# Norms of the later layers: squares added in pairs on GpSimd before TensorE sums them

## The reference

```python
def rms_norm(x, g):            # over the 1024 channels of each token
    return x * rsqrt(mean(x * x) + EPS) * g

for l in range(2):
    h = rms_norm(x, mix_pre_g[l])
    ...                        # latent attention, gating unit, differential attention
    x = x + rms_norm(mix, mix_post_g[l])
    h = rms_norm(x, mem_pre_g[l])
    x = x + rms_norm(memory_cross_attention(h, mem_n, ...), mem_post_g[l])
    h = rms_norm(x, ffn_pre_g[l])
    x = x + rms_norm(conv_ffn(h, ...), ffn_post_g[l])
```

## Time and profile before

| | |
|---|---|
| runs | 1940.42, 1940.86, 1935.62 us |
| median | 1940.42 us |
| profiled execution | 1938.43 us |
| its span, first to last instruction | 1936.6 us |
| mean granted TensorE clock | 0.967 of full |
| TensorE matmul busy | 1811.5 us |
| VectorE, ScalarE, GpSimd busy | 508.0, 422.8, 74.8 us |

### The profile page before, as it was taken

One profiled execution on the slowest core, in us unless ns is written; L12 is line 12 of the kernel. 1 busy time (PEld: TensorE's weight loads), 2 busy tenths in 40 slices (PEclk: granted clock), 3 DMA queues, 4 the chain that ended last, 5 costly groups with the idle time before them and its releaser, 6 DMA issues.

```text
span 1936.6 us, 24878 instructions
## 1 busy us (share of the span) xinstructions
PE 1811.5 (94%) x10310; PEld 1409.7 (73%) x10310; DVE 508.0 (26%) x1143; ACT 422.8 (22%) x907; POOL 74.8 (4%) x72
## 2 busy tenths in 40 slices
PE   4987878799999999999999999999999999899997
PEld 2674757566666665678678888888887688788886
DVE  3749432400100100022430312121135312212113
ACT  1532211211110110121442221111224522211112
POOL 0251000100000000010000100000000000000000
PEclk9988889799999999999999999999999999899999
DMA  9111256299999999983322323444433133234420
GB/s 393 41 44 44 82 224 261 111 398 422 422 422 422 422 421 422 422 332 134 123 85 109 130 106 134 152 152 152 151 137 131 44 130 109 87 131 152 152 87 22
DMA packets 53645, 383.32 MB, mean 198 GB/s; under 512 B 6208, under 2 KB 6336, under 8 KB 7360
## 3 DMA queue, kind: packets, MB, share of 16 engines
q1 hardware_dynamic: 52272, 376.97, 49.4%
q10 hardware_dynamic: 1296, 5.24, 0.7%
HBM read 381.14 MB, written 1.05 MB: 197 GB/s over the span
## 4 chain that ended last, share of the span: by engine, by line
PE 86%; DVE 6%; DMA 3%; ACT 2%; POOL 1%; issue 1%; SPq 0%; DVEq 0%; ACTq 0%
PE ps L576 83%; DMA ring<-in_stream 3%; PE ps L574 2%; PE ps L631 1%; DVE ring L1929 1%; POOL ring L460 1%; DVE arena L1935 1%; DVE arena L1929 1%; ACT arena L1693 0%; DVE small L2405 0%; DVE arena L1932 0%; DVE ring L2068 0%; ACT L1445 0%; DVE arena L2303 0%; DVE arena L1943 0%
## 5 line engine op out<-in xcount | busy, mean ns | idle before, releaser
L576 PE MATMUL ps<-arena,ring 128*128 128x256 f32 (+2 forms) x3680 | 833.7, 388 | 12.6 <-DVE arena L1932 5.8
L576 PEld LDWEIGHTS ps<-arena,ring 128*128 128x128 f32 x3680 | 697.1, 193 | 139.8 <-issue 46.7
L576 PE MATMUL ps<-ring,arena 128*64 128x256 f32 (+4 forms) x3168 | 485.0, 419 | 0.0
L576 PEld LDWEIGHTS ps<-ring,arena 128*64 128x64 f32 (+1 forms) x3168 | 294.1, 148 | 174.6 <-issue 84.5
L576 PE MATMUL ps<-arena 128*128 128x128 f32 (+5 forms) x1256 | 203.5, 322 | 6.9 <-DVE rounds_i L2259 2.2
L576 PEld LDWEIGHTS ps<-arena 128*128 128x128 f32 (+3 forms) x1256 | 167.4, 189 | 39.3 <-issue 24.5
L1935 DVE SCALAR_TENSOR_TENSOR arena<-ps,par,arena 128x255 f32<-128x255 f32 (+1 forms) x178 | 74.3, 479 | 336.7 <-ACT arena L1905 335.5
L576 PE MATMUL ps<-ring 128*128 128x256 f32 (+2 forms) x896 | 116.8, 302 | 12.6 <-DVE ring L2078 8.9
L576 PEld LDWEIGHTS ps<-ring 128*128 128x128 f32 (+2 forms) x896 | 99.4, 164 | 26.4 <-DVE ring L2078 9.7
L1905 ACT ACTIVATE arena<-ps,par 128x256 f32<-128x256 f32 x88 | 42.4, 563 | 313.5 <-PE ps L576 313.5
L576 PE MATMUL ps<-arena,cst 128*128 128x256 f32 (+1 forms) x308 | 88.6, 433 | 11.7 <-ACT arena L1721 5.4
(11 more groups left out here) (175 smaller groups left out, 796.3 us busy)
## 6 DMA issues: line engine op xcount, KB each, us to landing
ring<-in_stream SPq DMA_DIRECT2D x358, 1024.0 KB, 10.5
arena<-in_xc ACTq DMA_DIRECT2D x1, 1024.0 KB, 5.1
xT<-in_xc ACTq DMA_DIRECT2D x1, 1024.0 KB, 8.8
arena<-in_mem ACTq DMA_DIRECT2D x1, 1024.0 KB, 4.8
out_y<-xT ACTq DMA_DIRECT2D x2, 512.0 KB, 2.7
ring<-in_dft ACTq DMA_DIRECT2D x1, 512.0 KB, 8.0
arena<-in_sguw ACTq DMA_DIRECT2D x2, 256.0 KB, 2.8
par<-in_par SPq DMA_DIRECT2D x1, 511.5 KB, 24.6
```

The source lines that it names most:

```text
L576: i = nc.tensor.matmul(out, lhsT, rhs, start=start, stop=stop, skip_group_check=skip)
```

## The change

For norms 2 to 12 GpSimd adds squares together: chunks 2 and 3 onto chunks 0 and 1 (one instruction of 128x512), then chunks 4 and 5 onto the same two. TensorE then sums four tiles, 0, 1, 6 and 7, in place of eight. Norms 0 and 1 are as before. TensorE waits for GpSimd's second add (`xp_ok`) before tile 0, and for the squares of chunks 6 and 7. The sums that stood between the rounds of `out_proj` and in `down` are gone from there: all four are in the gap now. The last `mem_gain` stands behind the pair sums of norm 3.

```diff
+        xp_ok = sem("norm_pairs")
...
-            pool.wait_ge(late_ps, LATE_JOBS["kv_end0"])
-            mem_gain(memn, 1)
+
+            def pair_sums(k):
+
+                for c in (2, 4):
+                    pool.wait_ge(xq_ok, 8 * k + c + 2)
+                    i = tt(sq[:, 0:2, :], sq[:, 0:2, :], sq[:, c:c + 2, :], ALU.add)
+                    if c == 2:
+                        link(i)
+                i.then_inc(xp_ok, 1)
+
+            for k in range(2, 1 + 6 * LAYERS):
+                pair_sums(k)
+                if k == 3:
+                    pool.wait_ge(late_ps, LATE_JOBS["kv_end0"])
+                    mem_gain(memn, 1)
...
-            def sums(k, chunks):
-
-                for c in chunks:
-                    pe.wait_ge(xq_ok, 8 * k + c + 1)
+            def sums(k):
+
+                for c in range(KC) if k < 2 else (0, 1, 6, 7):
+                    if k < 2 or c > 1:
+                        pe.wait_ge(xq_ok, 8 * k + c + 1)
+                    else:
+                        pe.wait_ge(xp_ok, k - 1)
                     mm(bank(3, T), ones, sq[:, c, :], c == 0, c == KC - 1, xs_ps if c == KC - 1 else None)
...
                     release()
-                    if n:
-                        sums(k, (2 * n - 2, 2 * n - 1))
...
-                sums(k, (6, 7))
+                sums(k)
...
-                sums(k + 1, range(KC))
+                sums(k + 1)
...
-                        if i == FFN_PAIRS - 1 and o % 2 and o > 1:
-                            sums(n0 + 5, (o - 3, o - 2))
...
-                    sums(n0 + 5, (6, 7))
+                    sums(n0 + 5)
```

More of the change, by code:

```diff
@@ L1148, in _ @@
             mem_kv(0, 1, memn0, 1)
-            sums(0, range(KC))
+            sums(0)
             mem_kv(0, 1, memn0, 1)
-            sums(1, range(KC))
+            sums(1)
             mem_kv(0, KV_START - 2, memn0, 1)
```

## The result

The kernel with the change takes 1945.07 us, the median of 15 runs (1940.18 to 1949.20). The kernel before took 1935.86 us over 15 runs measured beside it (the three runs shown ahead of the prediction are among them). The ratio is 1.0047, 95% interval 1.0035 to 1.0059: 9 us more. I had forecast 1939.0 and no measurable difference, with the first median of 1940.42 as the base.

What follows compares the result with a forecast made beforehand. TensorE, busy 94% of the span, was taken to bound the kernel where it comes last. Terms of -4.1 us and +2.8 us for the clock gave -1.3 us: 1939.0 us forecast, range 1931.5 to 1946.5.

Steps and rivals of the forecast that it cites:

- What bounds the kernel, and the count of removed work: Whole kernel: TensorE bounds where it comes last; 44 matmuls of 0.43 us removed, 18.9 us of TensorE, not all on the path.
- y norm, filled: First norm of four pairs with memory projections as filling: root 2.6 us earlier, GpSimd's adds hidden by a projection round.
- x norm, filled: Second norm of those four pairs: GpSimd's adds stand on the path, 0.7 us gained each, -2.8 us in all.
- The port: SBUF port shared in x norms: GpSimd's add goes behind VectorE's current instruction, costing VectorE's row 0.7 us per add.
- Unfilled pair: Norms 10-11, without filling projections: first half gains 1.7 us, sums at half clock in the second, 0.4 us lost overall.
- Norm 12: Last norm, standing alone: last output 1.72 us earlier, sums end before the table load, 1.7 us gained.
- The clock: New 2.7 us TensorE waits in four filled pairs: one or two clock falls of 1.9 us each, +2.8 us.
- The sum: Terms before clock falls: -2.8 filled pairs, +0.4 unfilled pair, -1.7 norm 12, together -4.1 us.
- rival D: Filled pairs: clock falls in each and stays low for two stretches, +9.7 us, 1950; chance 0.10.
- E: Norm pairs: longer adds and VectorE losses cancel the gain from less TensorE work, 1940.0 us; chance 0.10.
- B: X norms: the port costs VectorE nothing, sum -8.3 us, 1932.1, or 1934 with a fall; chance 0.14.

Runs made afterwards that it cites:

- the y norms alone: GpSimd pair sums only in the six y norms, x norms as in the kernel before: 1924.65 us, ratio 0.9936.
- The runs with seams: The changed kernel with VectorE also waiting for its own adds to xT, after each add or only after chunk 4: both 1945.6 us, single runs.
- the kernel with filled waits: The changed kernel plus extra matmuls into an unused PSUM bank ahead of TensorE's wait for GpSimd in the x norms: 1938.04 us, ratio 1.0006.
- operands in PSUM: The changed kernel with VectorE's y-norm scale and add instructions each reading one operand from PSUM, gain and old trunk left out: 1929.62 us, ratio 0.9963.
- one seam: The changed kernel with VectorE also waiting for its add to chunk 4 before going on: 1945.6 us, a single run.
- GpSimd told to wait: The changed kernel with GpSimd also waiting for VectorE's last add to xT before its first x-norm pair add: 1945.27 us, ratio 1.0042.
- x norms alone: GpSimd pair sums only in the five x norms, y norms as in the kernel before: 1966.29 us, ratio 1.0145.

## Why the prediction was wrong, step by step

The step that failed is the x norm: GpSimd's first add was to be served behind VectorE's current instruction, at a price for VectorE. It was served only at the end of VectorE's row. The second term that was too small is the clock's.

- **What bounds the kernel, and the count of removed work: right.** 88 instructions fewer (10310 to 10222). TensorE is the late engine, and the y norms alone give 12 us with a calculated 10.3; what is above that is no more than the falls of the clock move from one execution to the next.
- **y norm, filled: right.** Forecast 2.6 us earlier for the root; from the last reciprocal ahead of it, it is 2.56 (1059.68 - 864.09 against 1061.97 - 863.82). The adds are hidden by the round.
- **x norm, filled: wrong, the step on the port.** I let GpSimd in behind VectorE's current instruction and charged VectorE 0.7 us for each add. It went the other way: VectorE lost nothing and GpSimd's first add waited for the whole row, 2.94 us. Both are signs of being wrong that I had named: no long VectorE add, and a GpSimd add of over 2 us. I had read the price of the contention from the earlier trace rows and the winner too, and only the price carries over to a row with seams. The second add was to end 3.1 to 3.5 us behind the request for the first one; it ended 4.28 us behind it. In the filled pair without a fall of the clock (below) the second reciprocal comes 12.20 us behind the first, where my forecast amounts to 9.52 + 2.58 - 0.7 = 11.4: 0.8 us mis-sized, four times 3.2 us.

```profile
1406.39 1.75 DVE L2316 RECIPROCAL arena<-arena 128x256 f32<-128x256 f32 x1 [12.92 <-ACT arena L1458]
...
1418.59 1.75 DVE L2316 RECIPROCAL arena<-arena 128x256 f32<-128x256 f32 x1 [4.96 <-ACT arena L1458]
```

- **The port.** The Trainium skill (SBUF — State Buffer, "SBUF: two separate sides") says that whoever starts first holds the shared pair for a whole instruction and that the other fully blocks. The runs agree with the blocking: 2.94 us with two SBUF operands on VectorE, 1.28 with one. I weighed it as a somewhat higher price for VectorE. The runs with seams show what comes of it in a row: between gapless instructions GpSimd isn't served before the row ends.
- **Unfilled pair: same error.** Forecast 0.4 us lost over both halves; 1.7 gained in the first and 3.4 lost in the second (13.99 - 10.56), so 1.7 lost, 1.3 more than forecast. The half clock on its four sums was in the forecast and came (3.78 us). Together with the filled pairs the port took 4.5 us of the forecast's -4.1, which leaves +0.4.
- **Norm 12: right.** 1.7 us (reciprocals 12 and 11 lie 235.63 us apart where they were 237.32). I had the sums end ahead of the table load; in both kernels they end while it runs, which costs nothing either.
- **The clock: right mechanism, wrong size.** I took one or two falls in the filled pairs at 1.9 us each, 2.8 us. The wait was 3.31 us and not 2.7, and the clock fell in three of four. Against the kernel with filled waits each fall cost 1.7 us; in the pair at 1155 it is 13.46 - 12.21 between the reciprocals and 0.4 in the stretch behind. That makes 5.1 us. Taking the idle time away gives 6.7 us of the late part back (1080.1 to 1073.4); the difference lies in the unfilled pair.
- **The sum.** -4.1 forecast, +4.5 port, +5.1 clock in the filled pairs come to +5.5 of a measured +7.3. Most of the rest is luck of the two profiled executions: in layer 1, between norms 7 and 8 and far from any of the new waits, the clock falls twice in the changed kernel and once in the kernel before, 1.7 us. The medians differ by 9.2 us; what they show beyond the 5.5 us stays open.
- **The range and the rivals.** 1945.07 lies inside 1931.5 to 1946.5, but the ratio is above the 0.3% bound, which rival D had with 0.10. D named the clock alone as the cause and needed long falls. Its deciding point, more than two ordinary falls, was passed. The case that came, a GpSimd add starved by VectorE with the falls behind it, was not among my rivals, since I had given VectorE the loss. B assumed that the port costs VectorE nothing and missed that it then costs GpSimd. The base also moved: the three runs shown before had a median of 1940.42, fifteen have 1935.86. That the time lies inside the range is luck of that base: counted from 1935.86, the upper end would have been 1941.9.
- **Small slips.** The wait of 1.85 us ahead of 977.40 is not one between transposes: twelve plain matmuls stand before it and four transposes behind it. E's terms come to 1939.8, not 1940.0, and D's four times 3.4 us to 13.6, not 13.8. Nothing hangs on them.

## What to carry to other kernels

Work moved to GpSimd is cheap where VectorE is idle and a job of TensorE covers it; all the gain of this change was there. Beside a gapless row of VectorE instructions with two SBUF operands it started only when the row ended, so count it from there. Before taking work off a busy TensorE ask whether the new wait leaves it idle: here 3.3 us of idling in four places brought three stretches at half clock, 5.1 us by the traces, and the adds' lateness cost 4.5.

## What the runs showed of the hardware

- GpSimd's 128x512 float32 add of two SBUF tiles takes 1.26 to 1.28 us alone, and 2.94 when asked for 1.8 us before the end of a VectorE row with two SBUF operands each. It ends 1.1 us behind the row. VectorE's 128x256 instructions stay at 0.42 us in that row.
- A seam of about 0.03 us between two VectorE instructions (1067.67 to 1067.70) is enough for GpSimd to go first. The VectorE instruction behind then takes 1.37 us in place of 0.42.
- With one operand in PSUM VectorE's instructions take the same 0.42 us, and GpSimd's add beside them takes 1.28 us.
- Of the four waits of TensorE in the filled pairs, the clock fell behind none when they were 1.65 us long (operands in PSUM), behind three when they were 3.0 (one seam) or 3.3 us (the change), behind all four at 3.5 (GpSimd told to wait) and at 4.1 us (x norms alone). A fall cost 1.7 us.
